# Nine of the first layer's twelve projections in three fp32r passes, with halves made by POOL, and a part of the constants loaded later

## The chip, the cores and the metric

The kernel runs on one core of a Trainium2 chip. A core has TensorE (PE, matrix products into PSUM banks), VectorE (DVE), ScalarE (ACT), GpSimd (POOL) and SyncE (SP), which issues most of the transfers from HBM. The metric is the device time of one execution in microseconds; lower is better. A text of times speaks of the median of several executions and, beside it, of the one execution that the profiler recorded.

## The reference, cut to what matters

Three blocks follow each other on x of 256 rows by 1024. All edits lie in the first:

```python
h = rmsnorm(x, g_pre)
proj = h @ w_in                      # (256, 1024) @ (1024, 6144)
q_a, k_a, v_a, g_a = ...             # columns 0..4095, 1024 each
x_m, z_m = ...                       # columns 4096..6143
o_a = moba_attention(q_a, k_a, v_a, rel_bias); y_a = o_a * silu(g_a)
x_c = silu(causal_depthwise_conv(x_m, conv_w, conv_b))
q_m, k_m = blockdiag(x_c), ...;  v_m = blockdiag(x_m, wv_m)
gates = concat(q_m, k_m, v_m) @ w_if + b_if
h_m = headwise_layernorm(mlstm(q_m, k_m, v_m, gates))
y_m = (h_m + skip * x_c) * silu(z_m)
x = x + rmsnorm(concat(y_a, y_m) @ w_out, g_post)
```

The second block takes six modulation vectors from `silu(c) @ ada_w`, a product of 1024 by 6144 for a single row, whose sums over the weights the kernel makes in the first layer's time.

## The kernel before, in words

**Projections.** `w_in` has twelve groups of 512 columns, in the order `B1_ORDER` (4096, 4608, 5120, 5632, 0, 512, ... 3584). `cols_T` (L718, products at L714) makes ten of them transposed: for each 256 columns a PSUM bank, two 128-column parts, eight products of 128x256 over the rows of `hT`. `cols_tok` (L724, L730) makes the groups 2048 and 2560, the values, token by token, with products of 128x512. All are plain fp32, straight from the weights as they landed. Each of these fp32 products stands as two records in the profile. Group 5120 is the last before the block-diagonal products (`bd`, L879 and L886), 5632 follows the gates, 0 to 1536 stand in the four heads of the mLSTM, 2048 and 2560 behind them, 3072 and 3584 in the attention (`B1_BETWEEN`).

**Ring.** SP issues all weights in one fixed order into `ring`, seven slots of 8 KB a partition (`piece`, L526). A group of columns is two pieces (rows 0 to 511 and 512 to 1023 of the weights); between two groups stand the two pieces of a group of `ada_w`, and the pieces of `w_out` at the end. The piece n is issued when piece n - 7 is used up.

**Modulation sums.** `ada_sum(x)` on VectorE (L2305, L2307) multiplies a group of `ada_w` by eight scalars and adds: eight operations of 128x512, the first with one tensor input, the others with two, both in SBUF. TensorE sums over the partitions (`ada_columns`, L846, and `ada_rows`, L854), and VectorE takes the result out of its bank (`ada`, L2319, L2322). In the mLSTM VectorE does, for each head: output of the head before (L2398 to L2401), masked logits and their maximum (L2374 to L2379), an `ada_sum`, the product with the scores (L2385) and the signal `probs_ready` (L2388), for which TensorE waits before it turns them (`turn_probs`, L794). After the four heads it normalises (L2407).

**Banks.** The small products and the projections share four PSUM banks in turn; `J.fill` waits until the bank's last content was taken out (`drained`).

**Constants.** One table of masks, tables and an identity: its first 256 columns come at once, the other 5339 by one transfer (L558) after the second group of weights. VectorE waits for it before it builds `bd` (L2346).

**Second layer.** Its projections already run in three fp32r passes (`in_half`, L750 to L758): the weight `w` is rounded to a high half, the low half is `w - high`, the same for the activations, and the product is high x high, high x low, low x high. ACT makes the high halves there, VectorE the low ones. The high and low halves lie over `bd` and in the arena.

**POOL** has almost nothing to do before: a few transfers and, after the heads, two small operations for the norm (L2991, L2992), waiting for `moments`. Every POOL and VectorE operation that goes through `do` is followed by a wait for its own end.

## Time and profile before

| | us |
|---|---|
| median of three executions | 2177.54 |
| lowest, highest | 2176.36, 2179.45 |
| the profiled execution, its own time | 2182.76 |
| its span | 2180.9 |
| TensorE busy | 2096.2 (96%) |
| VectorE busy | 1566.9 (72%) |
| ScalarE busy | 1251.5 (57%) |
| POOL busy | 16.9 (1%) |

The span is that of the instructions on the core; the time is some 2 us longer. The first layer ends at about 331 us of the span. TensorE's busy share is that of its records, whose ends are modelled, so durations of a group of products are best read from the start of one group to the start of what follows. The clock of TensorE is written as a share: 1.00 is 2.4 GHz, 0.50 is 1.2 GHz.

### The profile page before, as it was taken

Reading aid. Unit: us, or ns where it says so; the run is one execution under the profiler, and the core shown is the slowest. Engines: PE = TensorE matmul, PEld = TensorE weight load, DVE = VectorE, ACT = ScalarE, POOL = GpSimd, SP = SyncE. Lnnn points to the kernel's source line nnn. Section 1 sums busy time; section 2 is a strip of 40 time slices with the busy share of each in tenths; the row PEclk is TensorE's granted clock in tenths of the full one; section 3 lists DMA queues with packets and bytes.
Section 4 is the critical chain, followed back from the end, with each engine's and each line's share of the span. In section 5 each row is a group of like instructions: output and inputs, shape, how many; then the busy total and the mean of one; then the engine's idle time right before and its main releaser. Section 6 shows DMA issues by size and latency. Waiting matters only on the chain.

```text
span 2180.9 us, 30222 instructions
## 1 busy us (share of the span) xinstructions
PE 2096.2 (96%) x10504; PEld 1709.6 (78%) x10504; DVE 1566.9 (72%) x2095; ACT 1251.5 (57%) x1624; POOL 16.9 (1%) x31
## 2 busy tenths in 40 slices
PE   6999998889999999999998999999999999999998
PEld 5687657748998778998756888888888888888887
DVE  5346635676664764554257989999898989989897
ACT  2221226644444364443246877788787878878786
POOL 0000000000000000001000000000000000000000
PEclk9899999999999999999999999999999999999999
DMA  9557644236553316554315999999999999989995
GB/s 330 164 185 258 263 174 147 95 99 202 162 197 112 116 41 211 178 189 126 116 59 189 356 343 364 366 328 380 323 376 331 366 357 340 379 323 381 328 364 212
DMA packets 271918, 536.14 MB, mean 246 GB/s; under 512 B 29140, under 2 KB 80861, under 8 KB 271709
## 3 DMA queue, kind: packets, MB, share of 16 engines
q1 hardware_dynamic: 265917, 527.54, 67.7%
q10 hardware_dynamic: 5072, 4.36, 0.8%
q0 software_dynamic: 848, 3.15, 0.4%
q8 instruction: 52, 0.85, 0.2%
q14 instruction: 29, 0.24, 0.0%
HBM read 531.87 MB, written 3.14 MB: 245 GB/s over the span
## 4 chain that ended last, share of the span: by engine, by line
PE 89%; DVE 7%; ACT 2%; issue 1%; SPq 1%; DMA 1%; ACTq 0%; DVEq 0%
PE sum L1517 12%; PE bank L1499 9%; PE bank L1501 9%; PE bank L1500 9%; PE bank L714 9%; PE sum L1158 6%; PE sum L776 5%; PE bank L1175 3%; PE bank L1177 3%; PE bank L1176 3%; PE bank L1451 2%; PE bank L730 1%; PE sum L1265 1%; PE bank L1485 1%; PE sum L1531 1%
## 5 line engine op out<-in xcount | busy, mean ns | idle before, releaser
L2907 DVE TENSOR_TENSOR x_lo<-ring,x_hi 128x1024 fp32r<-128x1024 f32 x672 | 784.8, 1221 | 73.4 <-ACT x_hi L2059 48.6
L2059 ACT ACTIVATE x_hi<-ring 128x1024 fp32r<-128x1024 f32 x648 | 672.9, 1060 | 152.0 <-PE bank L1501 87.7
L1499 PE MATMUL bank<-x_hi,hg_hi 128*128 128x512 f32 x896 | 354.7, 396 | 1.5 <-DVE x_lo L2907 1.5
L1501 PE MATMUL bank<-x_hi,hg_lo 128*128 128x512 f32 x896 | 349.8, 390 | 0.0
L1500 PE MATMUL bank<-x_lo,hg_hi 128*128 128x512 f32 x896 | 349.1, 390 | 0.0
L2267 DVE TENSOR_TENSOR w_lo<-ring,w_hi 128x1024 fp32r<-128x1024 f32 x130 | 157.9, 1225 | 116.0 <-ACT w_hi L1869 114.3
L714 PE MATMUL bank<-hT,ring 128*128 128x256 f32 x1024 | 232.4, 389 | 2.3 <-DVE hT L2154 2.3
L714 PEld LDWEIGHTS bank<-hT,ring 128*128 128x128 f32 x1024 | 199.0, 195 | 35.1 <-issue 7.0
L1869 ACT ACTIVATE w_hi<-ring 128x1024 fp32r<-128x1024 f32 x130 | 136.8, 1060 | 147.6 <-PE bank L1177 76.3
L1501 PEld LDWEIGHTS bank<-x_hi,hg_lo 128*128 128x128 f32 x896 | 168.3, 188 | 36.0
L1499 PEld LDWEIGHTS bank<-x_hi,hg_hi 128*128 128x128 f32 x896 | 168.6, 188 | 35.2 <-DVE x_lo L2907 1.9
L1500 PEld LDWEIGHTS bank<-x_lo,hg_hi 128*128 128x128 f32 x896 | 168.8, 188 | 33.4
L1175 PE MATMUL bank<-hT_hi,w_hi 128*128 128x256 f32 x608 | 172.1, 283 | 1.5 <-DVE hT_lo L2251 0.9
L1177 PE MATMUL bank<-hT_hi,w_lo 128*128 128x256 f32 x608 | 172.1, 283 | 0.0
L1176 PE MATMUL bank<-hT_lo,w_hi 128*128 128x256 f32 x608 | 172.0, 283 | 0.0
L1600 ACT ACTIVATE arena<-bank 128x512 f32<-128x512 f32 (+3 forms) x81 | 46.2, 570 | 205.1 <-PE bank L714 98.2
L776 PE MATMUL sum<-ring,arena 128*128 128x512 f32 x304 | 135.5, 600 | 5.3 <-ACT arena L1958 2.1
L1175 PEld LDWEIGHTS bank<-hT_hi,w_hi 128*128 128x128 f32 x608 | 116.6, 192 | 3.2 <-issue 1.2
L1517 PE MATMUL sum<-x_hi,act_hi 128*128 128x512 f32 x384 | 119.0, 391 | 0.0
L1517 PE MATMUL sum<-x_lo,act_hi 128*128 128x512 f32 x384 | 118.3, 389 | 0.0
L1517 PE MATMUL sum<-x_hi,act_lo 128*128 128x512 f32 x384 | 118.3, 389 | 0.0
L1176 PEld LDWEIGHTS bank<-hT_lo,w_hi 128*128 128x128 f32 x608 | 116.6, 192 | 0.9
(481 smaller groups left out, 2849.5 us busy)
## 6 DMA issues: line engine op xcount, KB each, us to landing
ring<-in_sw_we_gate SPq DMA_DIRECT2D x114, 1024.0 KB, 6.9
ring<-in_sw_we_up SPq DMA_DIRECT2D x112, 1024.0 KB, 6.9
ring<-in_sw_we_down SPq DMA_DIRECT2D x112, 1024.0 KB, 6.8
ring<-in_w_in SPq DMA_DIRECT2D x36, 1024.0 KB, 7.5
ring<-in_w_ff SPq DMA_DIRECT2D x32, 1024.0 KB, 5.4
ring<-in_ada_w SPq DMA_DIRECT2D x24, 1024.0 KB, 7.2
ring<-in_w_out SPq DMA_DIRECT2D x12, 1024.0 KB, 7.3
ring<-in_cv_w_gate SPq DMA_DIRECT2D x11, 1024.0 KB, 5.2
```

Source lines behind the costliest of these rows:

```text
L714: last = mm(ps[b][:, j * S:(j + 1) * S], w[k][:, c0 + j * P:c0 + (j + 1) * P], hT[:, k, :], start=(k == 0), stop=(k == KC - 1))
L776: last = mm(acc[2 * t + h][:, :], mixT[:, 2 * k + j, t * P:(t + 1) * P], w[:, j, h * 512:(h + 1) * 512], start=(k == first and j == 0), st ...
L1175: mm(o, hi[:, k, cols], hT_hi[:, kk, :], start=(kk + j == 0), stop=False)
L1176: mm(o, hi[:, k, cols], hT_lo[:, kk, :], start=False, stop=False)
L1177: last = mm(o, lo[:, k, cols], hT_hi[:, kk, :], start=False, stop=(kk == KC - 1 and j == 1))
L1499: mm(ps[b][:, :], hg_hi[:, k, :], hi[:, cols], start=(k == 0), stop=False)
L1500: mm(ps[b][:, :], hg_hi[:, k, :], lo[:, cols], start=False, stop=False)
L1501: last = mm(ps[b][:, :], hg_lo[:, k, :], hi[:, cols], start=False, stop=(k == KC - 1))
L1517: last = mm(acc[h][:, :], a[:, k % 8, :], w[:, h * 512:(h + 1) * 512], start=(k == 0 and a is act_hi and w is hi), stop=(k == FFE // P - 1 ...
L2059: go(f(x_hi[:, hp % MSLOTS, :], ring[:, s, lo:lo + PIECE // 2], ACT.Copy), c.sig("hi_ready", hp))
L2267: v.tensor_tensor(w_lo[:, hp % SPLITS, :], ring[:, W.place(key), lo:lo + PIECE // 2], w_hi[:, hp % SPLITS, :].bitcast(F32), ALU.subtract). ...
L2907: v.tensor_tensor(x_lo[:, hp % MSLOTS, :], ring[:, s, lo:lo + PIECE // 2], x_hi[:, hp % MSLOTS, :].bitcast(F32), ALU.subtract).then_inc(c. ...
```

## The change

Nine groups of columns (`B1_SPLIT`: all but 4096, 4608 and 5120) go through a new `b1_group`, three passes from halves. POOL makes the halves, `h1_hi` and `h1_lo` of `hT` after group 5120 (the low ones over `hT` itself), then 36 halves of weights in the order of use: the high ones into three slots over `bd`, the low ones in place of the weights in the ring. Each group has four quarters (`half` in the code: two of the eight row blocks); quarter hp needs the half hp (`b1_lo`), and POOL may make half hp once quarter hp - 3 is used (`b1_used`). The group takes two banks at its start and fills both in step. The first piece of a group is free after its second quarter, the second after its fourth. The small norm operations of POOL stand between half 22 and half 23, a transfer between 33 and 34.

For room the constants are sorted: 2305 columns are wanted early (2049 of them in the large transfer), 3290 are `late`, where `h1_hi` lies until the last group is done. SP loads them after the last piece of `w_out`, behind a wait for the last quarter; TensorE and VectorE wait for `late_in` once, at the second layer's start.

```diff
+EARLY = ("ident", "ones", "upto", "causal", "block4", "rel", "hsel", "eps")
+B1_SPLIT = B1_ORDER[3:]
+B1_KEYS = [("w_in", col, h) for col in B1_SPLIT for h in range(2)]
...
-        consts = sb("consts", max(b for _, b in const_at.values()))
+        consts = sb("consts", n_early)
+        with ExitStack() as phase:
+            late = phase.enter_context(nc.sbuf_tensor("late", [P, n_consts - n_early], F32))
+        h1_hi = sb("h1_hi", KC, S, dt=F32R)
...
-        ring = sb("ring", RING, PIECE)
+        with ExitStack() as phase:
+            ring = phase.enter_context(nc.sbuf_tensor("ring", [P, RING, PIECE], F32))
+        ring_lo = sb("ring_lo", RING, PIECE, dt=F32R)
...
+        h1_lo = dT_hi
...
-                    sp.dma_start(consts[:, 2 * P:], A["consts"][:, 2 * P:]).then_inc(c.sem("consts_in"), 16)
+                    sp.dma_start(consts[:, 2 * P:], A["consts"][:, 2 * P:n_early]).then_inc(c.sem("consts_in"), 16)
...
             for k in (6, 7, 0, 1, 2, 3):
                 chunk_rows("w_out", A["w_out"][0], k)
+            sp.wait_ge(*W.half_used(len(B1_KEYS) * 2 - 1))
+            sp.dma_start(late[:, :], A["consts"][:, n_early:]).then_inc(c.sem("late_in"), 16)
...
+            def b1_group(col):
+                tok = col in (2048, 2560)
+                jobs = [("b1v", col, t) for t in range(NT)] if tok else [("b1p", col // 256 + q) for q in range(2)]
+                banks = [ps[J.fill(pe, *job)] for job in jobs]
+                for half in range(4):
+                    hp = 4 * B1_SPLIT.index(col) + half
+                    key = B1_KEYS[hp // 2]
+                    pe.wait_ge(*c.at("b1_lo", hp))
...
+                                for j in range(2):
+                                    y, cols = x[:, j * S:(j + 1) * S], slice(q * S + j * P, q * S + (j + 1) * P)
+                                    mm(y, hi[:, k, cols], h1_hi[:, kk, :], start=(kk + j == 0), stop=False)
+                                    mm(y, hi[:, k, cols], h1_lo[:, kk, :], start=False, stop=False)
+                                    last = mm(y, lo[:, k, cols], h1_hi[:, kk, :], start=False, stop=(kk == KC - 1 and j == 1))
...
-            cols_T("b1p", "w_in", 5632)
+            b1_group(5632)
...
-                    cols_T("b1p", "w_in", 512 * i)
+                    b1_group(512 * i)
...
-            cols_tok("b1v", "w_in", 2048)
+            b1_group(2048)
...
+            def b1_split(first, last):
+                for hp in range(first, last):
+                    key = B1_KEYS[hp // 2]
+                    if hp % 2 == 0:
+                        pool.wait_ge(*W.ready(key))
+                    if hp >= SPLIT_SLOTS:
+                        pool.wait_ge(*W.half_used(hp - SPLIT_SLOTS))
+                    o = (hp % 2) * (PIECE // 2)
+                    hi, w = d_hi[:, hp % SPLIT_SLOTS, :], ring[:, W.place(key), o:o + PIECE // 2]
+                    do(g.tensor_copy(hi, w))
+                    do(g.tensor_tensor(ring_lo[:, W.place(key), o:o + PIECE // 2], w, hi.bitcast(F32), ALU.subtract), c.sig("b1_lo", hp))
+
+            pool.wait_ge(*J.full("b1p", 21))
+            for k in range(0, KC, 4):
+                x, hi, lo = (y[:, k:k + 4, :].rearrange("p a b -> p (a b)") for y in (hT, h1_hi, h1_lo))
+                do(g.tensor_copy(hi, x))
+                do(g.tensor_tensor(lo, x, hi.bitcast(F32), ALU.subtract))
+            pool.wait_ge(*J.full("vm", 1, 1))
+            b1_split(0, 23)
             pool.wait_ge(*c.at("moments"))
...
+            b1_split(23, 34)
...
+            b1_split(34, 36)
```

Where the instructions stand. POOL, from its first transfer on, before:

```order
L2988 DMA arena<-in_ada_b 128x1024 [waits drained3,exponent]
L2991 ISA
L2991 TENSOR_SCALAR cmp<-cmp 128x8 [waits moments]
L2992 TENSOR_TENSOR cmp<-cmp,half_c 128x8 [waits pool_step]
L2994 DMA arena<-in_ada_b 128x1024 [waits filled1,rstd]
```

and now (`h_hi` is `h1_hi`, `dT_hi` holds `h1_lo` here, `d_hi` are the three high slots):

```order
L3044 DMA arena<-in_ada_b 128x1024 [waits drained3,exponent]
L3062 CAST h_hi<-hT 128x1024 [waits filled2]
L3063 ISA
L3063 TENSOR_TENSOR dT_hi<-hT,h_hi 128x1024 [waits pool_step]
L3062 CAST h_hi<-hT 128x1024 [waits pool_step]
L3063 TENSOR_TENSOR dT_hi<-hT,h_hi 128x1024 [waits pool_step]
L3056 CAST d_hi<-ring 128x1024 [waits landed5,filled3,pool_step]
L3057 TENSOR_TENSOR ring_lo<-ring,d_hi 128x1024 [waits pool_step]
L3056 CAST d_hi<-ring 128x1024 [waits b1_lo]
L3057 TENSOR_TENSOR ring_lo<-ring,d_hi 128x1024 [waits pool_step]
```

Between the first transfer and the norm stand now 4 operations on `hT` and 46 on weights (23 copies, 23 subtractions), each of 1024 elements in every partition.

TensorE, from the modulation column ahead of the turned mLSTM output to the start of group 2560, before:

```order
L846 MATMUL bank<-consts,junk 128x1 [waits drained1,ada_sum]
L846 MATMUL bank<-consts,junk 128x1 x3
L679 MATMUL bank<-consts,nrm 128x128 [waits drained2,normed]
L679 MATMUL bank<-consts,nrm 128x128 x3
L679 MATMUL bank<-consts,nrm 128x128 [waits drained3]
L679 MATMUL bank<-consts,nrm 128x128 x3
L730 MATMUL bank<-ring,hT 128x512 [waits drained0,landed2,landed1]
L730 MATMUL bank<-ring,hT 128x512 x7
L730 MATMUL bank<-ring,hT 128x512 [waits drained1]
```

and now:

```order
L698 MATMUL bank<-consts,nrm 128x128 [waits drained2,normed]
L698 MATMUL bank<-consts,nrm 128x128 x3
L698 MATMUL bank<-consts,nrm 128x128 [waits drained3]
L698 MATMUL bank<-consts,nrm 128x128 x3
L770 MATMUL bank<-d_hi,h_hi 128x512 [waits b1_lo,drained1,drained0]
L771 MATMUL bank<-ring_lo,h_hi 128x512
L772 MATMUL bank<-d_hi,dT_hi 128x512
```

The wait for bank 1, which the modulation column filled and VectorE empties, has moved from the middle of the group to its first product, beside the new wait for POOL's half.

## Rows read from the trace of the kernel before

**Rows 1.** TensorE's timeline: start, us, engine, line, operation, tiles, count, [idle before].

```profile
55.88 8.88 PE L865 MATMUL bank<-consts,logit 33*128 33x511 f32 x10 [6.34 <-DVE modc L2322]
```

**Rows 2.** Windows of TensorE: length, busy (count), granted clock, DMA share, GB/s.

```profile
49.50:55.80 6.30, 0.04 (x1) 0.50 1.05 411
55.80:64.70 8.90, 8.82 (x11) 0.50 0.59 228
64.70:81.20 16.50, 16.50 (x66) 0.84 0.64 128
```

**Rows 3.** VectorE's timeline, 26 to 56 us.

```profile
33.59 7.81 DVE L2346 TENSOR_TENSOR bd<-wraw,consts 128x128 f32<-128x128 f32 x24 [10.89 <-DMA consts<-in_consts]
...
55.66 0.16 DVE L2322 TENSOR_TENSOR modc<-bank,vcol 128x4 f32<-128x4 f32 x1
```

**Rows 4.** DMA issues, 0 to 60 us: size, us from issue to landing.

```profile
consts<-in_consts SPq DMA_DIRECT2D x1, 2669.5 KB, 14.6
```

**Rows 5.** TensorE's timeline, third mLSTM head (of four) to the attention.

```profile
163.85 13.98 PE L714 MATMUL bank<-hT,ring 128*128 128x256 f32 x64
177.67 0.95 PE L846 MATMUL bank<-consts,arena 128*128 128x1 f32 x8
178.48 0.53 PE L794 MATMUL bank<-consts,logit 128*128 128x128 f32 x3
...
200.07 13.90 PE L730 MATMUL bank<-ring,hT 128*128 128x512 f32 x32
213.80 0.95 PE L846 MATMUL bank<-consts,junk 128*128 128x1 f32 x8
...
215.52 13.90 PE L730 MATMUL bank<-ring,hT 128*128 128x512 f32 x32
...
239.17 13.98 PE L714 MATMUL bank<-hT,ring 128*128 128x256 f32 x64
```

**Rows 6.** TensorE's timeline, second layer's projections in three passes.

```profile
342.53 0.39 PE L756 MATMUL sum<-dT_hi,d_hi 128*128 128x256 f32 x1 [0.79 <-DVE dT_lo L2251]
...
365.67 0.40 PE L750 MATMUL sum<-d_hi,dT_hi 128*128 128x512 f32 x1
...
366.60 0.39 PE L751 MATMUL sum<-d_lo,dT_hi 128*128 128x512 f32 x1
```

**Rows 7.** POOL's groups of instructions: elements, count | busy us, mean ns | idle.

```profile
L3014 POOL TENSOR_SCALAR arena<-consts 128x384 f32<-128x384 f32 x12 | 6.1, 511 | 1.0
...
L2977 POOL TENSOR_SCALAR st<-st 128x4 f32<-128x4 f32 x2 | 0.4, 198 | 134.3 <-DVE st L2538 134.3
```

**Rows 8.** VectorE's timeline in the mLSTM and ahead of the attention.

```profile
115.14 5.47 DVE L2307 SCALAR_TENSOR_TENSOR junk<-ring,ccol,junk 128x512 f32<-128x512 f32 x7
...
124.31 0.41 DVE L2365 COPY aT<-bank 4x256 f32<-4x256 f32 x1 [1.23 <-PE bank L911]
...
166.45 5.48 DVE L2307 SCALAR_TENSOR_TENSOR junk<-ring,ccol,junk 128x512 f32<-128x512 f32 x7
...
172.77 0.17 DVE L2388 TENSOR_SCALAR mcol<-mcol 128x2 f32<-128x2 f32 x1
...
215.65 0.16 DVE L2322 TENSOR_TENSOR modc<-bank,vcol 128x4 f32<-128x4 f32 x1
...
235.43 0.69 DVE L2319 TENSOR_TENSOR arena<-arena,bank 128x512 f32<-128x512 f32 x1
```

**Rows 9.** Timeline of VectorE and POOL, 594 to 597 us.

```profile
594.14 1.23 DVE L2141 CUSTOM_DVE_ANT_0 junk<-arena 128x1024 f32<-128x1024 f32 x1
...
594.21 1.21 POOL L2977 TENSOR_SCALAR st<-st 128x1 f32<-128x1 f32 x1 [98.99 <-DVE st L2141]
...
596.16 0.19 POOL L2977 TENSOR_SCALAR st<-st 128x1 f32<-128x1 f32 x1
```

**Rows 10.** Timeline of POOL and VectorE, 465 to 467 us.

```profile
465.36 1.05 POOL L2978 TENSOR_TENSOR st<-st,half_c 128x4 f32<-128x4 f32 x1
...
466.01 0.35 DVE L2527 SCALAR_TENSOR_TENSOR arena<-arena,smx 128x128 f32<-128x128 f32 x1
```

More of the change, by code:

```diff
@@ L142, in constants @@
     at, out, n = {}, [], 0
+    parts = {k: parts[k] for k in EARLY + tuple(k for k in parts if k not in EARLY)}
     for k, a in parts.items():
@@ L272, in ffn_key, with half_used @@
         return (name, g) if name in ("ff2", "down") else (name, 256 * g, 0)
+    def half_used(self, hp):
+        name, v = self.known.halves["b1", hp] if self.known else ("b1_used", 1)
+        return self.c.sem(name), v
     def split_used(self, hp):
@@ L312, in sb @@
             return ctx.enter_context(nc.sbuf_tensor(name, [P, *shape], dt))
-        consts = sb("consts", max(b for _, b in const_at.values()))
+        n_early, n_consts = max(const_at[k][1] for k in EARLY), max(b for _, b in const_at.values())
+        consts = sb("consts", n_early)
+        with ExitStack() as phase:
+            late = phase.enter_context(nc.sbuf_tensor("late", [P, n_consts - n_early], F32))
+        h1_hi = sb("h1_hi", KC, S, dt=F32R)
+        sb("rest_of_late", n_consts - n_early - KC * S)
         def C(name, n=0):
             a, b = const_at[name]
-            v = consts[:, a:b]
+            v = consts[:, a:b] if name in EARLY else late[:, a - n_early:b - n_early]
             return v.rearrange("p (a b) -> p a b", a=n) if n else v
         ident, ones = C("ident"), C("ones")
-        ring = sb("ring", RING, PIECE)
+        with ExitStack() as phase:
+            ring = phase.enter_context(nc.sbuf_tensor("ring", [P, RING, PIECE], F32))
+        ring_lo = sb("ring_lo", RING, PIECE, dt=F32R)
         xres = sb("xres", NT, D)
@@ L732, in cols_tok @@
                 free(keys, s)
+            def b1_group(col):
[7 more added lines that the diff above has]
+                    o = (hp % 2) * (PIECE // 2)
+                    hi, lo = (w.rearrange("p (k n) -> p k n", k=2)
+                              for w in (d_hi[:, hp % SPLIT_SLOTS, :], ring_lo[:, W.place(key), o:o + PIECE // 2]))
+                    for q in range(2):
+                        for k in range(2):
+                            kk, x = 2 * half + k, banks[q]
+                            if tok:
+                                t = slice(q * P, (q + 1) * P)
+                                mm(x[:, :], h1_hi[:, kk, t], hi[:, k, :], start=(kk == 0), stop=False)
+                                mm(x[:, :], h1_hi[:, kk, t], lo[:, k, :], start=False, stop=False)
+                                last = mm(x[:, :], h1_lo[:, kk, t], hi[:, k, :], start=False, stop=(kk == KC - 1))
+                            else:
+                                for j in range(2):
[3 more added lines that the diff above has]
+                                    last = mm(y, lo[:, k, cols], h1_hi[:, kk, :], start=False, stop=(kk == KC - 1 and j == 1))
+                        if half == 3:
+                            s = done(last, *jobs[q])
+                    if half < 3:
+                        s = c.sig("b1_used", hp)
+                        last.then_inc(s.sem, 1)
+                    W.halves["b1", hp] = (s.name, s.base)
+                    if hp % 2:
+                        W.free(key, s)
             def in_half(hp):
@@ L950, in _ @@
             turn("mlstm", nrm, qs=(0, 1))
-            cols_tok("b1v", "w_in", 2560)
+            b1_group(2560)
             turn("mlstm", nrm, qs=(2, 3))
@@ L973, in b1_between @@
                 if i in B1_BETWEEN:
-                    cols_T("b1p", "w_in", B1_BETWEEN[i])
+                    b1_group(B1_BETWEEN[i])
                     ada_rows(9 + i // 2)
@@ L988, in _ @@
                 return
+            pe.wait_ge(c.sem("late_in"), 16)
             turn_x("mix2", (14, 5))
@@ L2470, in post1 @@
                 do(v.tensor_tensor(xres[:, t, cs], xres[:, t, cs], nrm[:, t, cs], ALU.add), c.sig("x_part", "mix2", 2 * t + h))
+            dve.wait_ge(c.sem("late_in"), 16)
             norm_x("mix2", post1, late=True)
@@ L2988, in _ @@
             pool.dma_start(gm, everywhere(A["ada_b_2"][:, 2 * D:3 * D], D)).then_inc(c.sem("gates_bias_in"), 16)
+            def b1_split(first, last):
[5 more added lines that the diff above has]
+                        pool.wait_ge(*W.half_used(hp - SPLIT_SLOTS))
+                    o = (hp % 2) * (PIECE // 2)
+                    hi, w = d_hi[:, hp % SPLIT_SLOTS, :], ring[:, W.place(key), o:o + PIECE // 2]
[8 more added lines that the diff above has]
+            b1_split(0, 23)
             pool.wait_ge(*c.at("moments"))
```

## The prediction

> **What bounds the kernel now.** I read the page's busy shares first: TensorE is busy for nearly all of the span, so time is won only by shorter TensorE work or by removing one of its few waits. Then I read TensorE's timeline of the first layer (0 to 331 us), where all edits lie. It holds twelve projections of 512 columns in plain fp32. One wait stands out: 6.34 us before 55.88, released by a VectorE write to `modc` [rows 1]. The granted clock there is 0.50, and it stays at that level (1.2 GHz) until some time into the third projection [rows 2]. Then I read VectorE's timeline for the cause: it sat idle for 10.89 us until the constants had landed, and from there its work follows without a gap up to the `modc` write at 55.66 [rows 3]. Those constants are 2669.5 KB, 14.6 us from issue to landing [rows 4].
>
> **Nine projections in three fp32r passes.** A projection lasts from 163.85 to 177.67 = 13.82 us in the 256-wide form, and from 200.07 to 213.80 = 13.73 us in the 512-wide one [rows 5]. The second layer already multiplies in three passes from halves. There 192 matmuls of 128x256 start between 342.53 and 365.67, so one takes 0.1205 us and a projection of 96 takes 11.57; the 128x512 ones start 0.2325 us apart (365.67 to 366.60, four steps), so 48 take 11.16 [rows 6]. Seven projections save 2.25 us each and two save 2.57: **-20.9 us**, if every half is ready and the clock stays up.
>
> **Fewer constants early.** 2049 of 5339 columns are left, 1024.5 KB; 1645 KB (1.68 MB) less. At the 411 GB/s that the queues move a little later [rows 2] this is 4.1 us, by which VectorE starts earlier on `bd`; its chain from there to `modc` has no idle time in it, and what it reads beside the constants (two evicted projections) is there before. TensorE's wait falls from 6.34 to about 2.2: **-4.1 us**, between nothing, should another load of that stretch be late next, and the whole 6.3. I give nothing for the clock: the first window at 0.50 starts at 49.5, where the wait has only begun, so what lowered it is the thin work ahead of it, and that stays. Were it kept up, 8.9 us at half speed and 16.5 at 0.84 [rows 2] would give back up to 4.4 + 2.6 = 7 us more. The late load (1.68 MB, 4 to 5 us of the queues) waits on SP for the last projection's last quarter. The `w_out` piece just ahead of it already waits for the same projection, so no load behind it starts later by the wait; the first second-layer weights are wanted some 45 us on, which hides the transfer.
>
> **Two banks at once.** A group now asks for both its banks at its start. For 2560 the second is the one that `ada(7)` leaves free, behind the normalising and a modulation sum on VectorE: emptied at 215.65 + 0.16 = 15.74 us after group 2048 started [rows 5, 8]. TensorE used to be there at 215.52, 15.45 after [rows 5], and is now there 2.57 earlier, at 12.88: **+2.9 us**. At the other groups that bank's last reader had finished before the group's start.
>
> **POOL makes the halves: its own pace.** No row shows POOL on 1024 elements. Its one-input operations take 511 ns for 384 elements and 198 ns for 4 [rows 7]: 0.82 ns an element, so 1.04 us for 1024, and 0.08 us between two. The subtraction reads two inputs; between one read (1.04) and three passes (2.72) I take two, 1.88, since the second input is what it adds to the copy. A half is then 1.04 + 1.88 + 2 x 0.08 = 3.08 us, 2.2 to 3.9 at the bounds. TensorE uses up a quarter in 2.9 us. Two groups of the mLSTM with the work between them last from 163.85 to 200.07, 18.1 us each, less 2.25 now: four halves (12.3 us) fit into 15.9. POOL alone is not late: only three high slots exist, so half 3 starts when quarter 0 is used, +2.9, is ready at +6.0 and wanted at +8.7. The split of `hT` (6 us) lies under the block-diagonal products.
>
> **POOL and VectorE together.** That is what decides. While the halves are made, VectorE sums modulation weights: eight operations a group, seven of them with two SBUF inputs, 0.78 us each [rows 8]. The trace shows what such an operation does to POOL: a POOL instruction on one column started at 594.21 and lasted 1.21 us, to the end of a VectorE operation on two SBUF inputs begun at 594.14; two microseconds later the same one lasted 0.19 [rows 9]. So they exclude each other, in that direction at least. For the other direction there is only a tiny sample: at 466.01 a two-input VectorE operation ran at its usual 0.35 us while POOL worked on four columns [rows 10]; those reads may have been over. I take it that a POOL operation which reads all along holds VectorE off too. Both engines wait for each operation's end before the next, so they take turns, and each VectorE operation waits for one of POOL's: 1.46 us on average (1.04 and 1.88).
>
> The Trainium skill (SBUF — State Buffer, Who interferes with whom) states this as an exclusive lock on a shared port pair, taken also by VectorE operations with two SBUF inputs against a POOL operation that reads SBUF, and held for the whole instruction; the 1.21 us row agrees, the 466.01 row doesn't show it. Another page (GPSIMD Engine Reference, Performance versus the Vector engine) has 4497 ns for a subtraction's like on 2048 elements, by which a turn would be about 1.65 us as an estimate and the result 8 us slower than mine; no row here shows it.
>
> Turns, place by place [rows 5, 8]:
> - Heads 1 to 3 of the mLSTM. VectorE starts its sum 2.1 us after the group (0.52 ahead of 166.45; 163.85), and POOL works from +2.9, so six operations meet one of POOL's: 6 x 1.46 = 8.8 us. `probs_ready` came at 172.77 + 0.17, +9.1, and comes at +17.9. TensorE used to reach the transposes at 178.48, +14.6, now +12.4: it waits 5.5 us, three times, 16.5. In head 0, with no output of an earlier head to write first, the sum starts 1.6 us earlier: 3.9.
> - Group 5632, ahead of the heads: all seven meet POOL, 10.2 us. VectorE ended the sum at 120.6 and took up the gates' rows at 124.31, 3.7 in hand, less 2.25: +8.8.
> - Before group 2560 (the 2.9 us above): six turns more, +8.8.
> - Before group 3072, whose second bank VectorE left free at 235.43 + 0.69 against a start at 239.17: six turns less 3.1 in hand, +5.7.
>
> Sum of the turns: **+43.7 us**. With the other terms: -20.9 - 4.1 + 2.9 + 43.7 = **+21.6 us**. The profiled execution took 2182.8 (span 2180.9), 5.2 above the median of the three runs shown, so 2204.4 on its scale and **2199** on the median's.
>
> **The rivals.**
> 1. Turns, as above. With the subtraction at 1.04 us a turn is 1.04 and the places give 5.9 + 10.0 + 6.2 + 3.2 = 25.3, the sum +3.2: 2181. With 2.72 a turn is 1.88 and they give 61.6, the sum +39.5: 2217; waits of six us and more may also lower the clock, as around 55.8 [rows 2], so up to 2222. For it: the 1.21 us row [rows 9]. Chance 0.58.
> 2. Side by side: POOL doesn't hold VectorE up, and is held up little itself. Then -20.9 - 4.1 + 2.9 = -22.1: **2155**, faster. For it: the 466.01 row, and the VectorE work that goes on undisturbed there. Against it: POOL's wait at 594.21 is the length of the VectorE operation, not a share of it. It decides for itself at the first modulation sum: 5.5 us for seven, or 15. Chance 0.25.
> 3. One-sided: VectorE isn't held up, POOL is, for all of each sum (6.0 us). Half 3 is then ready at 2.9 + 3.1 + 6.0 = +12.0 and wanted at +8.7: TensorE waits 3.3 us on `b1_lo` in each of nine groups, +29.7, against -22.1: +7.6, **2185**. Chance 0.12.
> 4. The change doesn't bring three-pass speed or the earlier start (halves late by POOL's own pace: beyond 4.0 us a half, four don't fit into 15.9 us), for a result near 2177. Chance 0.05.
>
> **How the numbers follow.** The likeliest case gives 2199, with its own range 2181 to 2222. It and the third case hold 0.70, so the range has to reach the second: 2152 to 2222. A measurement of this kernel can tell about 0.2% (4.4 us) from no change. Slower by more: nearly all of case 1, most of 3 and a part of 4, 0.69. Faster: case 2 and a little of 4, 0.26. Within: 0.05.
>
> **What would show each step.** In the profile of the changed kernel: matmuls of the nine groups 0.12 and 0.23 us apart; VectorE's `bd` some 4 to 5 us before 33.6, and the wait ahead of the bias table's products under 3 us; POOL's copies near 1.04 us and subtractions near 1.9 where VectorE is idle; the seven operations of a modulation sum at 2 us and more each instead of 0.75; TensorE waiting for `logit` or `mcol` of VectorE before the transposes, 4 to 6 us in each head. If those seven still last 0.75 us, case 1 is wrong; if TensorE then waits for `ring_lo`, it is case 3, if for nothing, case 2. If POOL's halves take over 4 us in quiet stretches, the pace I worked out is wrong.

## The result, and the profile after

The changed kernel takes 2210.66 us (median of four, 2205.47 to 2212.11), the kernel before 2178.24 (four, 2176.36 to 2179.45): a ratio of 1.014, 95% interval 1.0123 to 1.0157. It is slower, as the likeliest case of the prediction said, and by 32 us where that case gave 22. Its profiled execution took 2210.53 (span 2208.7), 27.8 above the profiled one of before. Of the runs below, the constants alone, again, had two executions of 6652.50 and 7458.11 us, the profiled one among them; its median leaves them out, and its trace is not used.

The page of the changed kernel, its busy shares and the engines on the chain that ended last:

```profile
PE 2091.8 (95%) x10760; PEld 1722.9 (78%) x10760; DVE 1638.8 (74%) x2095; ACT 1252.1 (57%) x1624; POOL 159.1 (7%) x107
...
PE 84%; DVE 11%; ACT 2%; issue 1%; SPq 1%; DMA 0%; ACTq 0%; POOL 0%; DVEq 0%; POOLq 0%
```

VectorE is busy 71.9 us longer, though the change gives it nothing to do, and its share of the chain is 11% instead of 7%. TensorE is busy 4.4 us less only, where its three-pass groups should have saved 21: part of that went to a lower clock, as is shown below.

**What went as forecast.** The groups: TensorE's timeline of group 5632 (start, us, engine, line, operation, tiles, count).

```profile
102.47 0.38 PE L776 MATMUL bank<-h_hi,d_hi 128*128 128x256 f32 x1
...
102.93 0.28 PE L776 MATMUL bank<-h_hi,d_hi 128*128 128x256 f32 x1
103.05 0.28 PE L777 MATMUL bank<-dT_hi,d_hi 128*128 128x256 f32 x1
103.17 0.29 PE L778 MATMUL bank<-h_hi,ring_lo 128*128 128x256 f32 x1
...
113.89 0.95 PE L900 MATMUL bank<-consts,junk 128*128 128x1 f32 x8
```

The products start 0.12 us apart, and from the first to what follows are 11.4 us (11.57 forecast, 13.82 in [rows 5]). The constants: VectorE's and TensorE's timelines ahead of the bias table, against 33.59 with 10.89 us of wait and 55.88 with 6.34 in [rows 1, 3].

```profile
28.98 7.78 DVE L2401 TENSOR_TENSOR bd<-wraw,consts 128x128 f32<-128x128 f32 x24 [6.20 <-DMA consts<-in_consts]
...
51.23 8.88 PE L919 MATMUL bank<-consts,logit 33*128 33x511 f32 x10 [1.40 <-DVE modc L2377]
```

The next row of modulation products starts at 75.70 instead of 81.18. The late load is issued at 302.99, and TensorE's wait at the second layer's first product is not longer for it (0.16 us, 0.79 before).

**Where the time went.** TensorE's waits of over 1 us from 100 to 300 us: who waited, for what, us in total, times, longest.

```profile
PE bank L848 <- DVE mcol L2443: 14.9, 2, 7.5
PE bank L981 <- DVE mcol L2423: 7.9, 1, 7.9
PE bank L698 <- DVE nrm L2462: 6.9, 1, 6.9
PE bank L770 <- issue: 4.3, 1, 4.3
PE bank L776 <- DVE arena L2475: 2.1, 1, 2.1
PE bank L1036 <- DVE arena L2475: 2.1, 1, 2.1
```

Before, the same stretch had not 1.5 us of waits. None is for a half of POOL's; all six name VectorE but the one called issue, and that one is the bank of `ada(7)`, which VectorE empties at 239.55. So look at VectorE (groups of instructions from 100 to 300 us: elements, count | busy us, mean ns | idle before):

```profile
L2362 DVE SCALAR_TENSOR_TENSOR junk<-ring,ccol,junk 128x512 f32<-128x512 f32 x33 | 54.8, 1661 | 1.2
L2362 DVE SCALAR_TENSOR_TENSOR arena<-ring,ccol,arena 128x512 f32<-128x512 f32 x28 | 40.4, 1443 | 1.0
L2462 DVE TENSOR_SCALAR nrm<-nrm,cmp 128x256 f32<-128x256 f32 x8 | 14.0, 1750 | 2.6 <-POOL cmp L3069 2.3
```

The two-input operations of the modulation sums took 752 ns before and take 1443 to 1661 on average. The normalising, one tensor input and two scalars, takes 1750 ns each where it took 413. The meeting itself, VectorE and POOL in the second head, from 148 to 157 us (the DVE row groups four operations):

```profile
148.36 1.04 POOL L3056 CAST d_hi<-ring 128x1024 fp32r<-128x1024 f32 x1 [0.22 <-PE bank L778]
148.45 8.57 DVE L2362 SCALAR_TENSOR_TENSOR arena<-ring,ccol,arena 128x512 f32<-128x512 f32 x4
149.48 2.73 POOL L3057 TENSOR_TENSOR ring_lo<-ring,d_hi 128x1024 fp32r<-128x1024 f32 x1
152.28 1.39 POOL L3056 CAST d_hi<-ring 128x1024 fp32r<-128x1024 f32 x1
```

Four operations that need 3.1 us take 8.57. By the chain of waits, the single ones here last 1.50, 2.80, 1.42, 2.79, 1.42 us in turn: each waits out one POOL operation. POOL loses less: 1.39 instead of 1.04 for a copy, 2.73 instead of 2.34 for a subtraction.

### The profile page after: what moved, and what is told of

Same layout as the page of the kernel before. It is cut to its first block, busy times and chain, and to the rows that moved or that the text cites. A ratio compares the mean times of both kernels' runs of the same rounds, so it can differ in the third digit from the quotient of the medians.

```text
span 2208.7 us, 30849 instructions
## 1 busy us (share of the span) xinstructions
PE 2091.8 (95%) x10760; PEld 1722.9 (78%) x10760; DVE 1638.8 (74%) x2095; ACT 1252.1 (57%) x1624; POOL 159.1 (7%) x107
## 4 chain that ended last, share of the span: by engine, by line
PE 84%; DVE 11%; ACT 2%; issue 1%; SPq 1%; DMA 0%; ACTq 0%; POOL 0%; DVEq 0%; POOLq 0%
PE sum L1572 12%; PE bank L1554 9%; PE bank L1556 9%; PE bank L1555 9%; PE sum L1213 6%; PE sum L830 5%; PE bank L733 4%; PE bank L1230 3%; PE bank L1232 3%; PE bank L1231 3%; DVE arena L2362 2%; PE bank L1506 2%; DVE junk L2362 1%; PE sum L1320 1%; PE bank L1540 1%
## 5 line engine op out<-in xcount | busy, mean ns | idle before, releaser
L733 PE MATMUL bank<-hT,ring 128*128 128x256 f32 x576 | 133.8, 395 | 2.3 <-DVE hT L2209 2.3
L733 PEld LDWEIGHTS bank<-hT,ring 128*128 128x128 f32 x576 | 113.6, 199 | 23.3 <-issue 7.0
```

Source lines behind the costliest of these rows:

```text
L733: last = mm(ps[b][:, j * S:(j + 1) * S], w[k][:, c0 + j * P:c0 + (j + 1) * P], hT[:, k, :], start=(k == 0), stop=(k == KC - 1))
```

## The experiments

| kernel | median us | ratio to the kernel before, measured beside it | 95% |
|---|---|---|---|
| changed kernel | 2210.66 | 1.0140 | 1.0123 to 1.0157 |
| before + later constants | 2178.63; again 2179.79 | 0.9987; 0.9985 | 0.9971 to 1.0002; 0.9974 to 0.9995 |
| short halves | 2158.87 | 0.9903 | 0.9870 to 0.9936 |
| POOL only writes | 2166.09 | 0.9925 | 0.9898 to 0.9952 |
| sums in PSUM | 2179.65 | 0.9994 | 0.9979 to 1.0008 |
| + heads in PSUM | 2162.44 | 0.9908 | 0.9891 to 0.9924 |
| filled waits | 2209.36 | 1.0123 | 1.0104 to 1.0141 |
| small pieces | 2184.41 | 1.0016 | 1.0006 to 1.0026 |
| all in PSUM | 2167.63 | 0.9942 | 0.9922 to 0.9962 |
| + mix in its bank | 2165.71 | 0.9924 | 0.9904 to 0.9943 |
| + sum 8 first | 2162.17 | 0.9909 | 0.9892 to 0.9926 |

Beside the experiments the kernel before had medians of 2179.75, 2182.90 and 2181.70 (17 to 20 executions each). All three are above the 2178.24 of the first four. Against them the changed kernel's 2210.66 is a loss of 27.8 to 30.9 us, so the true loss is more likely near 29 us than the 32.4 between the first medians.

**Constants alone.** The kernel before, with this of the change:

```diff
-                    sp.dma_start(consts[:, 2 * P:], A["consts"][:, 2 * P:]).then_inc(c.sem("consts_in"), 16)
+                    sp.dma_start(consts[:, 2 * P:], A["consts"][:, 2 * P:n_early]).then_inc(c.sem("consts_in"), 16)
...
+            sp.dma_start(late[:, :], A["consts"][:, n_early:]).then_inc(c.sem("late_in"), 16)
```

> The kernel before with one part of the change alone: 2049 constant columns early, 3290 behind the last piece of w_out. The changed kernel's trace has TensorE's wait ahead of the bias table at 1.40 us instead of 6.34, and what stands at 81.18 before starts at 75.70. If the part is worth what it shows there, 5.5 us: 2172 to 2174 (my prediction said 4.1 with nothing for the clock). Rival: the 5.5 us are eaten by a later wait in the first layer, since VectorE has its own list of work there: 2177 to 2178, and a new wait of TensorE between 76 and 165 us.

> The constants part alone once more, with more executions, since the first time gave -2.8 us with an interval of 6.3 to -0.4. Theory by its profile: TensorE's wait was 3.50 us (6.34 before), the first layer ended 3.0 us earlier: 2.5 to 3.5 us below the kernel before. Rival by the trace of the changed kernel (wait of 1.40): 5 us and more below. Third: nothing (within 1.5 us).

Measured: -2.8 us with an interval that reaches past nothing (0.4 slower), then -3.3 (0.0015 of 2182.9; 1.1 to 5.7). TensorE's timeline has

```profile
51.42 8.88 PE L870 MATMUL bank<-consts,logit 33*128 33x511 f32 x10 [3.50 <-DVE modc L2328]
```

so the product starts 4.5 us earlier than before, and the first layer ends 3.0 us earlier (333.87 against 336.85 for the turned x): the products of head 0 last 15.4 us there instead of 13.8, at a lowered clock (0.91 from 120 to 140 us). The part is worth about 3 us; the 4.1 that I took lies within the interval too.

**Is it POOL at all?** The changed kernel with

```diff
-                              for w in (d_hi[:, hp % SPLIT_SLOTS, :], ring_lo[:, W.place(key), o:o + PIECE // 2]))
+                              for w in (d_hi[:, hp % SPLIT_SLOTS, :], d_hi[:, hp % SPLIT_SLOTS, :]))
...
-                    do(g.tensor_copy(hi, w))
-                    do(g.tensor_tensor(ring_lo[:, W.place(key), o:o + PIECE // 2], w, hi.bitcast(F32), ALU.subtract), c.sig("b1_lo", hp))
+                    do(g.tensor_copy(hi[:, 0:8], w[:, 0:8]))
+                    do(g.tensor_tensor(hi[:, 8:16], w[:, 0:8], hi[:, 0:8].bitcast(F32), ALU.subtract), c.sig("b1_lo", hp))
...
+            for k in range(SPLIT_SLOTS):
+                do(g.tensor_copy(d_hi[:, k, :], ring[:, W.place(B1_KEYS[0]), 0:PIECE // 2]))
```

> The changed kernel, but POOL's two operations for a half of the weights work on 8 columns instead of 1024, and TensorE takes the high slot in the place of the low half too. So the weights of nine projections are left out of the result; all products, waits and signals stay. Theory (all of the loss is POOL's operations holding VectorE off): the waits of TensorE for VectorE (38.9 us from 100 to 270 us of the span) and the lowered clock behind them vanish, what is left is -20.9 for the passes, -5.5 for the constants and up to +2.9 for the two banks: 2154 to 2158. Rival (the new order, two banks asked for at once and the waits for halves cost of themselves): 2170 or more, with the waits before the turned tiles still there.

Measured 2158.87, 0.9 above the range that I gave. All products, signals and orders are as in the changed kernel (POOL fills the three high slots once, ahead of the first half), and 52 us of its 2210.7 are gone. TensorE's waits from 100 to 300 us are then

```profile
PE bank L770 <- issue: 3.0, 1, 3.0
PE sum L830 <- DVE arena L2497: 0.7, 1, 0.7
PE bank L981 <- DVE mcol L2423: 0.6, 1, 0.6
PE bank L955 <- ACT aT L1655: 0.6, 1, 0.6
```

and the sums' operations are back at 752 ns. The profiled executions differ by 23.2 us (2159.59 and 2182.76 before), the medians by 20.9, where the side-by-side case said 22.1. Three passes are worth what was worked out, and POOL's long operations cost all of the rest. The 3.0 us ahead of group 2560 are the second bank, 2.9 forecast.

**Reads or writes?** POOL fills the same two tiles with a constant:

```diff
-                    do(g.tensor_copy(hi, w))
-                    do(g.tensor_tensor(ring_lo[:, W.place(key), o:o + PIECE // 2], w, hi.bitcast(F32), ALU.subtract), c.sig("b1_lo", hp))
+                    do(g.memset(hi.bitcast(F32), 0.5))
+                    do(g.memset(ring_lo[:, W.place(key), o:o + PIECE // 2].bitcast(F32), 0.0), c.sig("b1_lo", hp))
```

> The changed kernel, but POOL fills the two tiles of a half with a constant (1024 columns each) instead of copying and subtracting, so it writes them and reads nothing; the weights of nine projections are left out of the result. Theory (VectorE's second input waits for POOL's reads alone): the operations of the modulation sums stay at 0.75 us although POOL is as often at work, and 2155 to 2170, with whatever POOL's writes do to the normalising. Rival (POOL's writes hold VectorE off as its reads do): the sums are stretched by one POOL operation each, 2185 to 2210 by how long such a fill takes.

Measured 2166.09, within the range. Timeline of both engines in the second head, and VectorE's groups:

```profile
139.19 5.48 DVE L2362 SCALAR_TENSOR_TENSOR arena<-ring,ccol,arena 128x512 f32<-128x512 f32 x7
140.97 0.96 POOL L3056 MEMSET d_hi<- 128x1024 f32 x1 [4.37 <-PE bank L778]
141.99 0.95 POOL L3057 MEMSET ring_lo<- 128x1024 f32 x1
```

```profile
L2462 DVE TENSOR_SCALAR nrm<-nrm,cmp 128x256 f32<-128x256 f32 x8 | 8.1, 1007 | 2.6 <-POOL cmp L3069 2.3
```

Seven two-input operations take 5.48 us, as before [rows 8], with two fills in their midst: writes of POOL don't touch them. They do touch the normalising, at 1007 ns instead of 413.

**One SBUF input instead of two.** The running sum lies in a PSUM bank that is idle until the output projection:

```diff
+                            part = acc[x % 4][:, :] if 3 <= x <= 8 else y
                             if h + k == 0:
-                                do(v.tensor_scalar(y, w[:, k, :], cond, None, ALU.mult))
+                                do(v.tensor_scalar(part, w[:, k, :], cond, None, ALU.mult))
                             else:
-                                do(v.scalar_tensor_tensor(y, w[:, k, :], cond, y, ALU.mult, ALU.add), s)
+                                do(v.scalar_tensor_tensor(y if h + k == 4 else part, w[:, k, :], cond, part, ALU.mult, ALU.add), s)
```

> The changed kernel, but the modulation sums 3 to 8 keep their running sum in a PSUM bank (the four sum banks are idle until the output projection) and write it to SBUF with the eighth operation, so that seven operations read one SBUF tensor instead of two. Theory (what holds VectorE off is its second SBUF input against POOL's reads): the operations last under 0.9 us again instead of 1.3 to 2.8, TensorE's waits of 7.94, 7.45 and 7.48 us go, and with them half of the clock's loss; the normalising (14.25 us) stays long. 2178 to 2187. Rival (any VectorE access of SBUF waits for POOL, one input or two): 2205 to 2212 as the changed kernel.

Measured 2179.65, within the range and 31 us less than the changed kernel, from an edit that changes no arithmetic. The groups of the same line in one kernel:

```profile
L2363 DVE SCALAR_TENSOR_TENSOR sum<-ring,ccol,sum 128x512 f32<-128x512 f32 x36 | 27.2, 756 | 1.3
L2363 DVE SCALAR_TENSOR_TENSOR junk<-ring,ccol,junk 128x512 f32<-128x512 f32 x14 | 21.4, 1530 | 0.5
L2363 DVE SCALAR_TENSOR_TENSOR arena<-ring,ccol,arena 128x512 f32<-128x512 f32 x7 | 15.2, 2177 | 0.2
L2463 DVE TENSOR_SCALAR nrm<-nrm,cmp 128x256 f32<-128x256 f32 x8 | 14.0, 1746 | 2.6 <-POOL cmp L3070 2.3
```

With the sum in PSUM 756 ns beside POOL at work; with the sum in SBUF (places 9 to 11, left as they were) 1530 and 2177. The three long waits in front of and in the heads are gone; the one for the normalising is still 6.9 us.

**The normalising.** On top of that, the heads' outputs are written to PSUM and normalised from there (the running sums 3 to 8 now share one bank):

```diff
+                            part = acc[3][:, :] if 3 <= x <= 8 else y
...
-                        x = nrm[:, t, h * MD:(h + 1) * MD]
+                        x = acc[h][:, t * S:(t + 1) * S]
...
-                    x, j = nrm[:, t, h * MD:(h + 1) * MD], 2 * (NT * h + t)
-                    do(v.tensor_scalar(x, x, moments[:, j:j + 1], moments[:, j + 1:j + 2], ALU.subtract, ALU.mult),
+                    x, y, j = nrm[:, t, h * MD:(h + 1) * MD], acc[h][:, t * S:(t + 1) * S], 2 * (NT * h + t)
+                    do(v.tensor_scalar(x, y, moments[:, j:j + 1], moments[:, j + 1:j + 2], ALU.subtract, ALU.mult),
```

> The run with the sums in PSUM (2179.7) and one thing more: the mLSTM's outputs are kept in PSUM and normalised from there, so that the eight normalising operations read PSUM and only write SBUF. The run in which POOL only writes had them at 1007 ns (414 undisturbed, 1750 against copies and subtractions), so POOL's writes alone hold them off while they go from SBUF to SBUF. Theory (an operation SBUF to SBUF takes a path that it shares with POOL, one from PSUM to SBUF doesn't): 0.4 to 0.5 us each, the wait of 6.9 us before the turned output shrinks under 1.5, 4.6 before group 2560 stays or grows by a part: 2170 to 2175. Rival (it is the write into SBUF that collides): about 1.0 us each or more, 2176 to 2180.

```profile
L2463 DVE TENSOR_SCALAR nrm<-sum,cmp 128x256 f32<-128x256 f32 x8 | 4.3, 543 | 2.6 <-POOL cmp L3070 2.3
```

543 ns instead of 1746, though it writes SBUF as before: the theory of the run holds, and the time, 2162.44, is some 8 us below its range. Three of four executions lie at 2162.3 to 2162.5 and the profiled one at 2171.94, within the range, so 2162 is not to be read finer than by its interval.

**The clock.** The waits sum to 38.3 us, but the stretch from group 5632 to the end of group 3072 lost 52 (below). I took the rest for the lowered clock, and put products on constants ahead of the long waits:

```diff
+            keep_busy(15)
             pe.wait_ge(*c.at("a_rows"))
...
                     ada_columns(3 + i)
+                    keep_busy(14 * (i % 2))
                     turn_probs("m", i, T384, i % 4)
...
+            keep_busy(13)
             pe.wait_ge(*c.at("normed", "mlstm"))
             turn("mlstm", nrm, qs=(0, 1))
+            keep_busy(8)
```

> The changed kernel with products on constants put ahead of TensorE's long waits (15 of 128x256 before the rows of the gates, 14 each before the turned tiles of heads 1 and 3, 13 before the turned mLSTM output, 8 before group 2560; 0.43 us each), so that it works while it waits for VectorE; nothing else moves. Theory (the waits lower TensorE's clock, and that is the part of the loss that the sum of waits, 38.9 us, doesn't hold, 10 to 13 us): the granted clock stays near 1.00 from 120 to 280 us, and the time falls to 2197 to 2203. Rival (the clock falls for another reason, or the added work lasts longer than the waits): the windows stay at 0.5 to 0.9, 2209 to 2216.

Measured 2209.36. Windows of TensorE (length, busy, granted clock, DMA share, GB/s), the changed kernel first, then the filled one:

```profile
120.00:140.00 20.00, 15.07 (x94) 0.74 0.38 134
...
160.00:180.00 20.00, 15.06 (x83) 0.68 0.37 129
```

```profile
120.00:140.00 20.00, 18.32 (x134) 1.00 0.44 151
...
160.00:180.00 20.00, 19.20 (x140) 1.00 0.51 174
```

Where the waits are filled the clock comes back, and the time doesn't: group 3072 starts at 268.18 in the one and 268.13 in the other. What the products save is waited for at the next place (4.9 us ahead of the transposes of head 2, where there was no wait), and there the clock falls instead (0.74 from 180 to 200 us, 1.00 in the changed kernel). Over the whole stretch it is 0.94 instead of 0.85, so the test is not a clean one; but the products that ran faster bought nothing. The half of my expectation that mattered, the time, fell: here the clock was a symptom. One more row tells why. The whole stretch, all engines, of the changed kernel (us, then PE, PEld, DVE, ACT and POOL busy):

```profile
102.47:281.20 178.73, 140.37 (x862) 122.79 (x861) 150.31 (x193) 24.00 (x46) 115.38 (x63) 0.85 0.56 190
```

and of the kernel before:

```profile
107.95:252.98 145.03, 144.38 (x638) 110.74 (x637) 86.71 (x195) 24.71 (x47) 1.92 (x2) 1.00 0.62 226
```

Before, TensorE is busy for all of it and VectorE for 87 us of 145. Now VectorE is busy for 150 of 179, longer than the whole stretch was, and TensorE for 140. I read this as a bound that has changed hands; the runs with PSUM bear it out, which shorten VectorE's operations alone and give 31 and 48 us.

**How long is one turn?** POOL's operations cut in two:

```diff
-                    do(g.tensor_copy(hi, w))
-                    do(g.tensor_tensor(ring_lo[:, W.place(key), o:o + PIECE // 2], w, hi.bitcast(F32), ALU.subtract), c.sig("b1_lo", hp))
+                    lo = ring_lo[:, W.place(key), o:o + PIECE // 2]
+                    for x in (slice(0, 512), slice(512, 1024)):
+                        do(g.tensor_copy(hi[:, x], w[:, x]))
+                        do(g.tensor_tensor(lo[:, x], w[:, x], hi[:, x].bitcast(F32), ALU.subtract), c.sig("b1_lo", hp) if x.start else None)
```

> The changed kernel, but POOL makes each half in two pieces of 512 columns (four operations instead of two). VectorE's operation waits for the end of one POOL operation, whichever is under way, and then takes 0.55 us more. Theory (the price is the length of the other's instruction): about 1.0 and 1.7 us instead of 1.42 and 2.8, a disturbed sum of seven 9 to 10 us instead of 14 to 15, TensorE's long waits 3 to 5 us shorter in four places, though POOL's halves take longer: 2188 to 2200. Rival (a fixed price for each meeting of the two engines, or VectorE slowed by the share of time that POOL reads): the sums stay at 14 us and more, 2207 to 2215.

Measured 2184.41, below the range I gave. The sum of head 1, 14.20 us in the changed kernel, is now

```profile
146.35 9.79 DVE L2362 SCALAR_TENSOR_TENSOR arena<-ring,ccol,arena 128x512 f32<-128x512 f32 x7
```

POOL works on the same elements, in pieces of half the size, and the kernel is 26 us shorter: the price is the length of the other's instruction, not its work. Single operations of that sum last 0.98 us beside a copy of 0.95 and 1.67 beside a subtraction of 1.62. POOL needs longer for a half in all (a copy of 512 lasts 746 ns on average, a subtraction 1413), and now TensorE waits 5.3 us for its halves. For VectorE it still waits 18.5 us, 9.7 of them ahead of group 2560, where sum 8 now meets POOL too (9.68 us instead of 5.48).

**A version that beats both.** From the heads in PSUM I went on: sum 9 in PSUM too, `ada(7)` ahead of sum 8, POOL's norm behind half 23.

> The changed kernel with what the runs so far point to, nothing left out: the running sums 3 to 9 in one PSUM bank (TensorE waits for sum 9 before its first output projection), the heads' outputs written to PSUM and normalised from there into SBUF, the result of ada(7) taken out ahead of sum 8 instead of behind it, and POOL's small norm operations behind half 23 instead of ahead of it. Theory: TensorE's waits that the run with sums in PSUM still has (6.9 before the turned mLSTM output, 4.6 before group 2560, 2.3 and 2.6 in the attention, 1.0 for a half) go, and with them the clock they cost: 2155 to 2162, at or under the run with short halves (2158.9), since that one still had 3.0 us before 2560. Rival (other operations with two SBUF inputs or SBUF to SBUF copies take over as the late ones): 2165 to 2175.

Measured 2167.63, in the range of the rival and not better than the heads in PSUM alone. Its profile has two new waits. VectorE waited 5.05 us for POOL's norm, which I had moved behind a half. And TensorE waited for `mix_heads`, whose operations between SBUF tensors had begun to meet POOL (VectorE from 203 to 207 us, and TensorE behind it):

```profile
203.21 2.07 DVE L2477 TENSOR_TENSOR arena<-arena,junk 128x256 f32<-128x256 f32 x1
205.31 1.01 DVE L2475 TENSOR_SCALAR junk<-arena,vcol 128x256 f32<-128x256 f32 x1
206.35 0.48 DVE L2476 SCALAR_TENSOR_TENSOR junk<-bank,vcol,junk 128x256 f32<-128x256 f32 x1
...
216.21 1.12 PE L698 MATMUL bank<-consts,nrm 128*128 128x128 f32 x4 [6.49 <-DVE arena L2477]
```

The three rows of VectorE are three operations of that chain, one after the other: two SBUF inputs 2.07 us (0.42 undisturbed), SBUF to SBUF 1.01 (0.35), one SBUF and one PSUM input 0.48, undisturbed. So the next one takes the norm back and builds the mixed output in its own bank:

```diff
...
-                    x = junk[:, j * S:(j + 1) * S]
-                    do(v.tensor_scalar(x, xcT[:, k, :], vec("skip", k), None, ALU.mult))
-                    do(v.scalar_tensor_tensor(x, b[:, j * S:(j + 1) * S], vec("mh_norm", k), x, ALU.mult, ALU.add))
+                    x = b[:, j * S:(j + 1) * S]
+                    do(v.tensor_scalar(x, x, vec("mh_norm", k), None, ALU.mult))
+                    do(v.scalar_tensor_tensor(x, xcT[:, k, :], vec("skip", k), x, ALU.mult, ALU.add))
```

> The run with all sums and heads in PSUM (2167.6), changed in the two places that its trace shows late: POOL's norm operations are back ahead of half 23 (VectorE waited 5.05 us for them), and the gated mLSTM output is built in its own PSUM bank, so that none of its three operations reads two SBUF tensors or goes from SBUF to SBUF (they took 1.01 and 2.08 us instead of 0.35 and 0.42, and TensorE waited 6.49 us for them). Theory: the waits of 6.49 and 3.50 us behind group 2560 go, 1 to 2 us before its turned input stay: 2155 to 2160. Rival (the extra work in PSUM banks or sum 9 is late next, TensorE waits 3 us or more there again): 2161 to 2166.

> As the run before in this call, but sum 8 ahead of the result of ada(7), as in the changed kernel. This costs only the bank that group 2560 asks for at its start. Theory: VectorE empties it one sum later, TensorE waits about 2.9 us there (2.97 and 2.92 in the two runs with undisturbed sums) and not for VectorE afterwards, so the difference is 1 to 3 us: 2157 to 2162. Rival: no difference or faster, since VectorE does not idle for TensorE's column before sum 8: 2153 to 2157.

Measured 2165.71 and 2162.17. The first kept a wait of 3.7 us for sum 9 ahead of the attention, and lies where its rival said; the second, at the upper end of its range, with sum 8 ahead of `ada(7)` as in the changed kernel, has 2.92 us ahead of group 2560 and 1.06 for a half, and no other wait of a microsecond in the stretch. Its first layer hands over the turned x at 314.58 instead of 336.85. At 0.9909 (0.9892 to 0.9926) it beats the kernel before by some 20 us and the changed one by 48. It is not told apart from the heads in PSUM alone (0.9908).

## Why the prediction was right, and what it missed

**Direction and mechanism.** The deciding step, that a POOL operation which reads SBUF holds off a VectorE operation with two SBUF inputs, was drawn from one POOL row of the other direction [rows 9] and against one of VectorE [rows 10]. The short halves and the sums in PSUM show it from both sides. The Trainium skill (SBUF — State Buffer, Who interferes with whom) states it so, reads against reads, and the runs agree: 752 ns beside POOL's fills, up to 2.8 us beside its copies and subtractions. Its word that the other engine "fully blocks" fits both ways: VectorE's operation lasts until POOL's has ended, and POOL's copy at 152.28, begun with 0.50 us of a VectorE operation to go, grew by 0.35 us.

**The size of a turn.** 1.46 us were forecast; seven disturbed operations took 15.42 us at most (at 246.48) against 5.48, 1.42 each. The subtraction takes 2.34 us undisturbed, within the bounds (1.04 to 2.72) and above the 1.88 I chose, the copy 1.04 as forecast. A half is 3.5 us, 4.3 disturbed, and no wait of TensorE names POOL, so the third and fourth case don't hold; the second falls with VectorE's 1661 ns.

**The places.** They were near only as a sum (us of TensorE's wait, forecast and found), and that the total came near is in part luck: the waits were put 8.3 us too high, and a larger loss that the sum had no term for stood against it (below).

| | 5632 | head 0 | head 1 | head 2 | head 3 | before 2560 | before 3072 | sum |
|---|---|---|---|---|---|---|---|---|
| forecast | 8.8 | 3.9 | 5.5 | 5.5 | 5.5 | 8.8 + 2.9 | 5.7 | 46.6 |
| found | 7.9 | 0 | 7.5 | 0 | 7.5 | 6.9 + 4.3 | 4.2 | 38.3 |

Two steps of the working failed. First, I took every head for the same. After a long wait of TensorE POOL has its three slots full and stands still, until TensorE uses one; VectorE's next sum begins in that quiet time. The sums show it (timelines of VectorE and POOL: the sums of heads 0 to 3 with POOL's first operation after each of two long pauses, the normalising, sum 8):

```profile
128.96 6.15 DVE L2362 SCALAR_TENSOR_TENSOR arena<-ring,ccol,arena 128x512 f32<-128x512 f32 x7
...
133.53 1.04 POOL L3056 CAST d_hi<-ring 128x1024 fp32r<-128x1024 f32 x1 [12.25 <-PE bank L778]
...
148.45 14.20 DVE L2362 SCALAR_TENSOR_TENSOR arena<-ring,ccol,arena 128x512 f32<-128x512 f32 x7
...
173.19 8.81 DVE L2362 SCALAR_TENSOR_TENSOR junk<-ring,ccol,junk 128x512 f32<-128x512 f32 x7
...
175.85 1.35 POOL L3056 CAST d_hi<-ring 128x1024 fp32r<-128x1024 f32 x1 [11.00 <-PE bank L778]
...
192.19 14.11 DVE L2362 SCALAR_TENSOR_TENSOR junk<-ring,ccol,junk 128x512 f32<-128x512 f32 x7
...
219.23 14.25 DVE L2462 TENSOR_SCALAR nrm<-nrm,cmp 128x256 f32<-128x256 f32 x8 [2.31 <-POOL cmp L3069]
...
234.04 5.48 DVE L2362 SCALAR_TENSOR_TENSOR arena<-ring,ccol,arena 128x512 f32<-128x512 f32 x7
```

Second, I counted turns for operations with two tensor inputs only. Sum 8, to which I gave the 8.8 us before group 2560, met nobody (5.48); it was the normalising ahead of it, one input, SBUF to SBUF, that took 14.25 us instead of 3.56. The same section of the Trainium skill names `tensor_scalar` among the operations that can take the shared ports, and makes for them no condition on POOL's reads, as it does for two inputs. The runs agree: 1007 ns beside fills, 1750 beside reads, 543 from PSUM. I had weighed its sentence on two inputs and not that one.

**The sum.** From group 5632 to the end of group 3072 the kernel before took 145.03 us, the changed one 178.73. The eight groups in it save 6 x 2.25 + 2 x 2.57 = 18.6, so 52.3 were lost there, 5.7 more than the 46.6. Read from TensorE, they are the 38.3 us of waits and some 14 by which its products took longer: it was busy for 140.4 us where 144.4 - 18.6 = 125.8 were due, at a granted clock of 0.85 instead of 1.00. Since the filled waits raised that clock and won nothing, I put the difference down to the model: I added waits of a TensorE that stays the bound, and it doesn't stay so. With VectorE as the bound, the added VectorE time counts (150.3 - 86.7 = 63.6 us busy) less what slack it had; no run measures that slack. The rest: the constants gave 5.5 in this execution (1.4 more than forecast), the later layers 2.1 us more without a cause that I can name, and the profiled execution of before lay 4.5 above its median, that of after 0.1 below. 21.6 + 5.7 - 1.4 + 2.1 + 4.6 = 32.6, and 32.4 were measured.

**The constants** stayed in their bounds (0 to 6.3), and alone are worth about 3 us. **The clock** I left out of the likeliest case. It fell around the long waits, to 0.74 and 0.68 in the windows above, and giving it back there moved nothing; so the choice was right, though not for a reason that I had. The prediction also used [rows 2] both ways, once as a clock lowered by the work ahead of the wait and once as a case of a wait that lowers it.

## What to carry to other kernels

Before an idle GpSimd is given work on SBUF, list what VectorE does at that time by operands: two SBUF inputs, or a TENSOR_SCALAR from SBUF to SBUF. Each such operation waited until the GpSimd instruction under way had ended, however small it was itself, so as an estimate the cost is their number times the length of the other's instruction. Not every operation with one SBUF input is hit: beside POOL's subtractions (189.00 to 191.40 and 185.47 to 187.82 us) two TENSOR_REDUCE took their usual 0.74 us together and a BATCH_NORM_STATS2 its 0.43. Keep the running operand of VectorE in an idle PSUM bank, or cut GpSimd's work into shorter instructions; and once an engine's busy time in a stretch comes near to the stretch, stop adding up the waits of the one that was the bound.

## What the runs showed of the hardware that I had not expected

- A VectorE operation on two columns waited as long as a large one. `L2443 TENSOR_SCALAR mcol<-mcol 128x2` took 1426 ns on average (0.17 us before [rows 8]), and with the sums in PSUM a two-column subtraction took 2.28 us instead of 0.16.
- Each engine waited for what the other had left of its operation, so the one with the shorter operations lost more. VectorE's two-input operation lasted until POOL's ended and 0.55 us more (152.21 and 152.78 in the second head), and POOL's next was lengthened by 0.35 to 0.39 us. Beside the normalising, whose operation ended 0.15 us after POOL's (220.38 and 220.23), POOL's copies took their 1.04 us and its subtractions 2.34 to 2.40.
- One PSUM operand was enough to be free of POOL, as an input (756 ns against 1530 to 2177 on one line) or as the only tensor input of an operation that writes SBUF (543 ns against 1746).
- POOL's writes alone more than doubled the one-input TENSOR_SCALAR from SBUF to SBUF (1007 ns, 413 undisturbed) and left the two-input ones at 752.
- TensorE's clock stood at 1.00 where its waits were filled with products (120 to 140 and 160 to 180 us, 0.74 and 0.68 without them), and the kernel was not faster for it.
